# Four split buffers, four opening quarters, a queue of its own for the first weights, and the last two value units made 512 wide

## The chip, the cores and the metric

The kernel runs on one core of a Trainium2 chip. The time is that of one execution on the device, in microseconds (us); less is better. Engines are named as in the profile: PE (TensorE, matrix products), DVE (VectorE), ACT (ScalarE), POOL (GpSimd), SP (SyncE, which issues the transfers).

## What is computed

One decoder layer over 256 tokens of width 1024, in float32, and a last RMS norm:

```python
def layer(h, mem):
    u = rms_norm(h, norm_mix)
    z = u @ w_in                                   # 1024 x 3328
    y_rwkv = rwkv7_time_mix(z[:, :1792], ...)      # 8 heads x 64, a recurrence over tokens, group norm, gate
    q, k, v = split(z[:, 1792:], 3)
    y_moba = causal_softmax_attention(q, k, v)     # 8 heads x 64 (one block of 256 tokens)
    h = h + concat([y_rwkv, y_moba]) @ w_mix_out
    q = rms_norm(h, norm_xattn) @ w_xq             # 4 heads x 256
    k, v = split(rms_norm(mem, norm_mem) @ w_xkv, 2)
    h = h + softmax(q @ k.T / 16) @ v @ w_xo
    a = square(relu(rms_norm(h, norm_ffn) @ w_ff1))   # 1024 x 4096
    h = h + a @ w_ff2
    return rms_norm(h, norm_final)
```

## The kernel before, in words

**Split products.** Each weight product is made of three matmuls of rounded operands: high x high, high x low and low x high. A weight goes through three places: a transfer brings a unit of 1 MB into one of three `raw` buffers (`load_unit`, SP); ACT rounds half a unit, 128x1024, into `w_hi` (`split_hi`); DVE subtracts it from the original to get `w_lo` (`split_lo`). There are `NSPLIT` = 3 such pairs, used in turn: half `s` can be rounded only when half `s - 3` has been multiplied (`dense_mm`).

**Units and quarters.** `units()` lists the 65 units in the order in which they are loaded: `z` (input projection of the recurrence), `mq` and `mv` (attention), `xk` and `xw`, `xv` (keys and values of the cross-attention), `mix` (w_mix_out), `xq`, `xo`, `f1`, `f2`. PE works in quarters of a unit, 260 in all, in the order of `QUARTERS`; 12 matmuls of 256 columns, or 6 of 512 in the `WIDE` units. The letter a below stands for the first half of the inner dimension and b for the second. The first two units of `mix`, of `xo` and of `f1` are interleaved: two quarters that need only the part of the input which is ready early come first, and the ones that need the late part (`dve_gate`, `dve_values`, `dve_op`) behind them.

**Order on each engine.** Each engine has one instruction stream, written out by hand: `dense(n)` on PE is the next n quarters, `split()` on ACT and DVE the next half, and between them stand the steps of everything else. The recurrence goes through `lora`, `rates`, `sums`, `key_sums`, `key_norm`, `decays`, `keys`, `tails`, `tokens`, `bonus`, `mats`, `invert`, `cross`, `join`, `solve`, `outq`, `phi`, `psi`, `state`, `states_out`, `deviation`, `head_root`, `normalize` and `gate`; the attention through `pair_...`; the cross-attention through `scores`, `weigh`, `turn`, `values`. `take(o)` is DVE's emptying of an output's PSUM bank, `operand(what, j)` the rounding of two of the eight slices of the input of the next product (ACT high, DVE low), `rms` the norm. `load(0, q)` transposes a quarter of x and `first_hi`/`first_lo` split the first unit by quarters. From the first `f1` unit on, ACT's and DVE's streams follow from the quarters by a rule.

## Time and profile before

| | |
|---|---|
| three runs | 479.34, 481.86, 481.69 us; median 481.69 us |
| profiled execution, time | 479.82 us |
| its span (first to last instruction) | 477.7 us |
| mean granted clock of PE | 0.998 |
| PE busy | 452.7 us (95%) |
| DVE busy | 321.8 us (67%) |
| ACT busy | 246.5 us (52%) |
| a split, half a unit | ACT L992 1.05 us, DVE L1314 1.25 us (means of 128) |
| `operand`, one of two instructions | ACT L1033 0.50 us, DVE L1403 0.75 us (means of 16) |
| an emptying: h (L1357), `xw` (L1364), half an `xv` (L1370) | 0.68, 0.75, 0.47 us |
| `sums` (L1475, L1477) | 2.28 and 1.23 us |

PE carries the products without a break in most of the span; a product's issue is the thing to look at, since a matmul's shown length overlaps the next one's. The span begins with the loading of x and ends with the last norm and the stores.

### The profile page before, as it was taken

The numbers are of one execution on the slowest core, as the hardware profiler recorded it, in microseconds if no ns is written. First come the engines' busy times: TensorE is split into PE (matmuls) and PEld (weight loads), VectorE is DVE, ScalarE is ACT, GpSimd is POOL, SyncE is SP. The second block draws the span as 40 slices with busy tenths as digits, with TensorE's granted clock in tenths as the row PEclk, the third lists the DMA queues.
The fourth block names the chain that finished last, engine by engine and source line by source line (L and its number), as shares of the span: only waits on it lengthen the run. The fifth ranks groups of instructions, "written<-read, shape, count | busy, mean of one in ns | idle before, by whom it ended". The sixth has DMA issues, their size and how long they took to land.

```text
span 477.7 us, 10346 instructions
## 1 busy us (share of the span) xinstructions
PE 452.7 (95%) x4390; PEld 404.3 (85%) x4390; DVE 321.8 (67%) x475; ACT 246.5 (52%) x396; POOL 35.2 (7%) x54
## 2 busy tenths in 40 slices
PE   4999999999899999899999997999999999999995
PEld 3999999878788888899998995888888888888883
DVE  3667899985567948569476367575747575666656
ACT  4799944245464446337344344555544354544444
POOL 8300000000000000052000053000000000000000
PEclk9999999999999999999999999999999999999999
DMA  8953464222422415454443155446565746657412
GB/s 247 308 186 114 151 195 149 92 92 80 124 93 89 126 59 170 137 171 159 153 155 111 50 144 160 157 140 231 177 196 161 245 151 217 199 197 230 142 69 88
DMA packets 59937, 73.05 MB, mean 153 GB/s; under 512 B 1378, under 2 KB 48564, under 8 KB 59892
## 3 DMA queue, kind: packets, MB, share of 16 engines
q1 hardware_dynamic: 59812, 72.14, 46.7%
q8 instruction: 35, 0.57, 0.5%
q0 software_dynamic: 80, 0.26, 0.2%
q14 instruction: 10, 0.08, 0.1%
HBM read 71.35 MB, written 1.05 MB: 152 GB/s over the span
## 4 chain that ended last, share of the span: by engine, by line
PE 71%; DVE 12%; ACT 5%; issue 3%; ACTq 0%; DVEq 0%
PE bank L542 9%; PE bank L556 7%; PE bank L558 7%; PE bank L557 7%; PE bank L593 6%; PE bank L595 6%; PE bank L594 6%; PE bank L540 5%; DVE w_lo L1314 4%; DVE op L1403 2%; PE bank L573 2%; ACT w_hi L992 2%; PE bank L575 2%; PE bank L574 2%; PE bank L917 2%
## 5 line engine op out<-in xcount | busy, mean ns | idle before, releaser
L1314 DVE TENSOR_TENSOR w_lo<-raw,w_hi 128x1024 fp32r<-128x1024 f32 x128 | 158.9, 1251 | 76.6 <-ACT w_hi L992 76.3
L992 ACT ACTIVATE w_hi<-raw 128x1024 fp32r<-128x1024 f32 x128 | 133.2, 1054 | 70.1 <-PE bank L558 28.2
L556 PE MATMUL bank<-op,w_hi 128*128 128x256 f32 x416 | 121.4, 292 | 4.5 <-DVE w_lo L1314 2.8
L558 PE MATMUL bank<-op,w_lo 128*128 128x256 f32 x416 | 117.8, 283 | 1.1 <-issue 1.1
L557 PE MATMUL bank<-op,w_hi 128*128 128x256 f32 x416 | 117.6, 283 | 0.0
L556 PEld LDWEIGHTS bank<-op,w_hi 128*128 128x128 f32 x416 | 79.5, 191 | 7.6 <-issue 6.2
L558 PEld LDWEIGHTS bank<-op,w_lo 128*128 128x128 f32 x416 | 79.6, 191 | 1.5 <-issue 1.5
L542 PE MATMUL bank<-op,w_hi 128*128 128x512 f32 x224 | 80.0, 396 | 0.0
L557 PEld LDWEIGHTS bank<-op,w_hi 128*128 128x128 f32 x416 | 79.7, 191 | 0.2
L540 PE MATMUL bank<-op,w_lo 128*128 128x256 f32 x256 | 66.4, 280 | 0.1
L540 PEld LDWEIGHTS bank<-op,w_lo 128*128 128x128 f32 x256 | 48.3, 189 | 2.9 <-DVE op L1403 0.4
L593 PE MATMUL bank<-w_hi,op 128*128 128x512 f32 x128 | 50.0, 391 | 0.4 <-DVE w_lo L1314 0.4
L595 PE MATMUL bank<-w_hi,op 128*128 128x512 f32 x128 | 49.8, 389 | 0.0
L594 PE MATMUL bank<-w_lo,op 128*128 128x512 f32 x128 | 49.8, 389 | 0.0
L542 PEld LDWEIGHTS bank<-op,w_hi 128*128 128x128 f32 x224 | 42.1, 188 | 8.6
L1041 ACT ACTIVATE op<-s 128x512 fp32r<-128x512 f32 x16 | 10.1, 632 | 42.4 <-DVE s L1417 42.4
L593 PEld LDWEIGHTS bank<-w_hi,op 128*128 128x128 f32 x128 | 24.0, 188 | 5.8 <-issue 0.8
L595 PEld LDWEIGHTS bank<-w_hi,op 128*128 128x128 f32 x128 | 24.0, 188 | 5.1
L594 PEld LDWEIGHTS bank<-w_lo,op 128*128 128x128 f32 x128 | 24.0, 188 | 5.0
L1420 DVE TENSOR_TENSOR op<-s,op 128x512 fp32r<-128x512 f32 x16 | 11.1, 693 | 11.2 <-ACT op L1041 11.2
L539 PE MATMUL bank<-op,w_hi 128*128 128x512 f32 x32 | 13.1, 410 | 3.3 <-DVE w_lo L1314 2.0
L1050 ACT ACTIVATE s<-bank 128x256 f32<-128x256 f32 x32 | 10.9, 372 | 8.3 <-PE bank L542 8.3
(258 smaller groups left out, 606.4 us busy)
## 6 DMA issues: line engine op xcount, KB each, us to landing
raw<-in_w_ff SPq DMA_DIRECT2D x32, 1024.0 KB, 5.5
raw<-in_w_in SPq DMA_DIRECT2D x12, 1024.0 KB, 5.4
raw<-in_w_xkv SPq DMA_DIRECT2D x8, 1024.0 KB, 5.3
raw<-in_w_mix_out SPq DMA_DIRECT2D x4, 1024.0 KB, 5.0
raw<-in_w_xq SPq DMA_DIRECT2D x4, 1024.0 KB, 5.0
raw<-in_w_xo SPq DMA_DIRECT2D x4, 1024.0 KB, 4.9
xval<-in_x SPq DMA_DIRECT2D x4, 256.0 KB, 4.8
raw<-in_w_in SPq DMA_DIRECT2D x4, 256.0 KB, 5.5
```

The source lines that it names most:

```text
L539: mm(pair(b[:, :]), wh[:, k, :], op[0][:, :, k, :], start=True, stop=False)
L540: mm(b[:, 0:T], wl[:, k, :], op_hi[0][:, k, :], start=False, stop=False)
L542: last = mm(pair(b[:, :]), wh[:, k, :], op[0][:, :, k, :], start=False, stop=final)
L556: mm(dst, wh[:, k, :], op_hi[which][:, k, :], start=first, stop=False)
L557: mm(dst, wh[:, k, :], op_lo[which][:, k, :], start=False, stop=False)
L558: last = mm(dst, wl[:, k, :], op_hi[which][:, k, :], start=False, stop=final)
L593: mm(dst[:, :], hi, wh[:, k, :], start=first, stop=False)
L594: mm(dst[:, :], hi, wl[:, k, :], start=False, stop=False)
L595: last = mm(dst[:, :], lo, wh[:, k, :], start=False, stop=final)
L992: op(view(w_hi), r, ACT.Copy).then_inc(hi_done, 1)
L1314: tt(view(w_lo), r, view(w_hi).bitcast(f32), ALU.subtract).then_inc(lo_done, 1)
L1420: tt(op_lo[1][:, k:k + 2, :], pair(sq), op_hi[1][:, k:k + 2, :].bitcast(f32), ALU.subtract).then_inc(dve_hidden, 1)
```

## The change

The change does five things. The four transfers of the first unit are issued by ACT instead of SP. `NSPLIT` becomes 4; the room comes from `tmp`, half of `rinv` and `center`, which move into buffers that are free at the time. The three opening pairs of units take four early quarters before the first late one, with PSUM room for four half outputs (`half_of_out`). The two `xv` units, one ahead of `mix` and one behind it, become two `xx` units of 512 columns, both behind `mix`. POOL squares the new h after `operand` instead of after `take`. The streams of PE, ACT and DVE are written anew around this.

```diff
-NRAW, NSPLIT = 3, 3
+NRAW, NSPLIT = 3, 4
...
-    out += [("xv", "w_xkv", 0, D + 512, 2)]
     out += [("mix", "w_mix_out", 0, 256 * j, j) for j in range(4)]
-    out += [("xv", "w_xkv", 0, D + 256 * j, j) for j in range(3, 4)]
+    out += [("xx", "w_xkv", 4 * j, D + 512, j) for j in range(2)]
...
-WIDE = ("mv", "xw")
+WIDE = ("mv", "xw", "xx")
...
-        QUARTERS += [(2 * _u + _i, _late ^ _p ^ 1) for _i, _p in
-                     ((0, 0), (2, 0), (0, 1), (1, 0), (1, 1), (2, 1), (3, 0), (3, 1))]
+        QUARTERS += [(2 * _u + _i, _late ^ _p ^ 1) for _p in range(2) for _i in range(4)]
...
+        def half_of_out(o, i):
+
+            what, j = OUTS[o][3:5]
+            if i and j < 2 and what in ("mix", "xo"):
+                return B[{"mix": 4, "xo": 2}[what] + j][:, 0:T]
+            return dense_bank[o % 2][:, i * T:i * T + T]
...
-                sp.dma_start(first_to[:, k, :], first[:, k, UNITS[0][3]:UNITS[0][3] + 256]).then_inc(first_in[i], 16)
...
-                    pool.wait_ge(out_taken, FIRST[what] + j + 1)
+                    if what == "mix":
+                        pool.wait_ge(dve_op, op_no("mix", j) + 1)
+                    elif j == 0:
+                        pool.wait_ge(dve_op, op_no("xo", 3) + 1)
...
-            params(0); load(0, 0); load(0, 1); load(0, 2); dense(1); load(0, 3); dense(2); params(1); dense(1)
-            spread(0); dense(4); lora(); dense(9); key_sums(); dense(4); spread(1); dense(12); load(1, 0)
-            dense(2); tokens(); load(1, 1); dense(1); bonus(); values_turn(); dense(1); mats(0); dense(2)
...
+            params(0); load(0, 0); load(0, 1); dense(1); load(0, 2); dense(1); load(0, 3); dense(2); params(1)
+            spread(0); dense(8); lora(); dense(8); key_sums(); dense(2); spread(1); dense(11); load(1, 0)
+            tokens(); dense(1); load(1, 1); bonus(); values_turn(); dense(1); mats(0); dense(1); load(1, 2)
...
-            pair_scores(2); state(2); dense(4); pair_turn(2, 0); pair_turn(2, 1); state(3); pair_values(2)
...
-            pair_turn(3, 1); states_out(); dense(2); deviation(); dense(4); gate(); dense(3); pair_values(3)
-            dense(22); rms(2); dense(6); scores(0); dense(3); scores(1); turn(0); dense(2); values(0); turn(1)
...
+            pair_turn(3, 0); pair_turn(3, 1); states_out(); dense(2); deviation(); dense(3); pair_values(3)
+            gate(); dense(30); rms(2); dense(4); scores(0); dense(2); scores(1); turn(0); dense(2); values(0)
...
+            for i in range(4):
+                k = slice(2 * i, 2 * i + 2)
+                act.dma_start(first_to[:, k, :], first[:, k, UNITS[0][3]:UNITS[0][3] + 256]).then_inc(first_in[i], 16)
             act.wait_ge(pool_const, 1)
...
+                    if j < 2:
+                        tt(h[:, 0, :], half_of_out(o, 0), h[:, 0, :], ALU.add)
+                        tt(h[:, 1, :], half_of_out(o, 1), h[:, 1, :], ALU.add).then_inc(out_taken, 1)
+                        return
                     tt(h, src, h, ALU.add).then_inc(out_taken, 1)
```

The quarters stand so on PE. At `mix`, before: mix0 first half b, mix1 first half b, then mix0 first half a, which waits for the gates. Now: both halves of mix0 and of mix1 with b, and then the four with a. `xo` and `f1` are built alike, with a first and b late. In front of the gates PE had 76 quarters and two early ones of `mix`; now it has 72 and four. `tokens` stood behind quarter 34 and stands behind quarter 32, `mats(0)` behind 36 and now behind 34, `deviation` behind 71 and now behind 70.

**ACT, the opening.** The first instructions of ACT before (L1063 and L983 are `load(0, q)` with `first_hi(q)`, L1084 and L1090 are `stats(0)`, L992 is a `split`, L1073 is `copies`):

```order
L970 ACT_TABLE_LOAD
L970 ACTIVATE small<-eps 128x1
...
L1063 ACTIVATE op0<-bank2,par 128x256 x2
L983 ACTIVATE w_hi<-raw 128x512
L1063 ACTIVATE op0<-bank3,par 128x256 x2
L983 ACTIVATE w_hi<-raw 128x512
L1084 ACTIVATE neu,row_sum<-xval 128x1024 x2
L1090 ACTIVATE row_sum<-row_sum,eps 128x2
L992 ACTIVATE w_hi<-raw 128x1024
L1073 ACTIVATE hT<-bank0 128x512
```

And now, where L1066, L986, L1087, L1093, L995 and L1076 are the same in turn:

```order
L970 DMA raw<-in_w_in 128x2x256 x4
L973 ACT_TABLE_LOAD
L973 ACTIVATE small<-eps 128x1
...
L1066 ACTIVATE op0<-bank2,par 128x256 x2
L986 ACTIVATE w_hi<-raw 128x512
L1076 ACTIVATE hT<-bank0 128x512
L1076 ACTIVATE hT<-bank1 128x512
L1066 ACTIVATE op0<-bank3,par 128x256 x2
L986 ACTIVATE w_hi<-raw 128x512
L1087 ACTIVATE neu,row_sum<-xval 128x1024 x2
L1093 ACTIVATE row_sum<-row_sum,eps 128x2
L995 ACTIVATE w_hi<-raw 128x1024 x2
```

The four transfers stand first, and the copies of the first two quarters of x have moved from behind `stats(0)` to ahead of the last quarter's rounding.

**DVE, from the norm of the recurrence to the gates.** Before (L1648 and L1651 are `normalize`, L1657 is `gate`, L1661 is `gate_low`, L1686 is `pair_values(3)`, L1370 empties the first `xv` unit, L1364 an `xw` output):

```order
L1364 TENSOR_SCALAR xval<-bank,row_sum 128x512
L1314 TENSOR_TENSOR w_lo<-raw,w_hi 128x1024
L1648 SCALAR_TENSOR_TENSOR s<-s,par 128x256 x4
L1651 TENSOR_TENSOR s<-s 128x1024
L1657 TENSOR_TENSOR s<-bank,s 128x512 x2
L1314 TENSOR_TENSOR w_lo<-raw,w_hi 128x1024
L1661 TENSOR_TENSOR op<-s,op 128x512
L1314 TENSOR_TENSOR w_lo<-raw,w_hi 128x1024
L1686 TENSOR_TENSOR op<-bank,op 128x256
L1370 TENSOR_SCALAR xval<-bank,row_sum 128x256 x2
L1314 TENSOR_TENSOR w_lo<-raw,w_hi 128x1024
L1661 TENSOR_TENSOR op<-s,op 128x512
```

And now (L1374 empties an `xw` output, L1651 and L1654 are `normalize`, L1689 `pair_values(3)`, L1660 `gate`, L1664 `gate_low`, L1319 a split, L1363 and L1364 empty mix0):

```order
L1374 TENSOR_SCALAR xval<-bank,row_sum 128x512
L1651 SCALAR_TENSOR_TENSOR s<-s,par 128x256 x4
L1654 TENSOR_TENSOR s<-s 128x1024
L1689 TENSOR_TENSOR op<-bank,op 128x256
L1319 TENSOR_TENSOR w_lo<-raw,w_hi 128x1024
L1660 TENSOR_TENSOR s<-bank,s 128x512
L1374 TENSOR_SCALAR xval<-bank,row_sum 128x512
L1660 TENSOR_TENSOR s<-bank,s 128x512
L1319 TENSOR_TENSOR w_lo<-raw,w_hi 128x1024 x2
L1664 TENSOR_TENSOR op<-s,op 128x512 x2
L1363 TENSOR_TENSOR hT<-bank,hT 128x256
L1364 TENSOR_TENSOR hT<-bank,hT 128x256
```

`normalize` no longer stands behind the second emptying of `xw` and a split, `pair_values(3)` has moved ahead of the gates, and the emptying of `xv` is gone from here.

**DVE, from the last `xo` outputs into `f1`.** Before (L1357 empties an `xo` output into hT, L1403 is the low part of `operand`, L1314 is a split):

```order
L1314 TENSOR_TENSOR w_lo<-raw,w_hi 128x1024
L1357 TENSOR_TENSOR hT<-bank,hT 128x512
L1314 TENSOR_TENSOR w_lo<-raw,w_hi 128x1024
L1403 SCALAR_TENSOR_TENSOR op<-hT,par,op 128x256 x2
L1314 TENSOR_TENSOR w_lo<-raw,w_hi 128x1024
L1357 TENSOR_TENSOR hT<-bank,hT 128x512
L1314 TENSOR_TENSOR w_lo<-raw,w_hi 128x1024
L1403 SCALAR_TENSOR_TENSOR op<-hT,par,op 128x256 x2
L1314 TENSOR_TENSOR w_lo<-raw,w_hi 128x1024
```

And now (L1366, L1406 and L1319 are the same in turn):

```order
L1319 TENSOR_TENSOR w_lo<-raw,w_hi 128x1024 x2
L1366 TENSOR_TENSOR hT<-bank,hT 128x512
L1319 TENSOR_TENSOR w_lo<-raw,w_hi 128x1024
L1406 SCALAR_TENSOR_TENSOR op<-hT,par,op 128x256 x2
L1319 TENSOR_TENSOR w_lo<-raw,w_hi 128x1024
L1366 TENSOR_TENSOR hT<-bank,hT 128x512
L1319 TENSOR_TENSOR w_lo<-raw,w_hi 128x1024
L1406 SCALAR_TENSOR_TENSOR op<-hT,par,op 128x256 x2
L1319 TENSOR_TENSOR w_lo<-raw,w_hi 128x1024 x3
```

The order reads much alike; what differs is which half each split is. Ahead of the emptying of the last `xo` output (the second L1366) the first two halves of `f1` are now split, where before it was the first alone; the third follows between that emptying and its operand, and the fourth right behind the operand.

## Rows read from the trace of the kernel before

**Rows 1.** The page, part 1: busy time of each engine

```profile
PE 452.7 (95%) x4390; PEld 404.3 (85%) x4390; DVE 321.8 (67%) x475; ACT 246.5 (52%) x396; POOL 35.2 (7%) x54
```

**Rows 2.** Busy time by stretch: us, PE, PEld, DVE, ACT, POOL, clock, DMA

```profile
40.00:60.00 20.00, 19.12 (x150) 18.60 (x151) 14.50 (x22) 19.35 (x27) 0.00 (x0) 1.00 0.38 115
60.00:80.00 20.00, 19.73 (x160) 19.18 (x159) 19.79 (x26) 8.60 (x15) 0.00 (x0) 1.00 0.44 149
```

**Rows 3.** Timeline of PE: start, length, line, operation; products of 256 columns

```profile
199.84 0.28 PE L558 MATMUL bank<-op,w_lo 128*128 128x256 f32 x1
199.96 0.28 PE L556 MATMUL bank<-op,w_hi 128*128 128x256 f32 x1
```

**Rows 4.** Timeline of PE, products of 512 columns (unit `xw`)

```profile
173.12 0.40 PE L575 MATMUL bank<-w_hi,op 128*128 128x512 f32 x1
173.35 0.40 PE L573 MATMUL bank<-w_hi,op 128*128 128x512 f32 x1
```

**Rows 5.** Timeline, the opening; in brackets idle time before and its releaser

```profile
6.05 0.88 DVE L1445 SCALAR_TENSOR_TENSOR op<-bank,par,op 128x256 fp32r<-128x256 f32 x2 [2.03 <-ACT op L1063]
...
8.92 1.12 PE L643 MATMUL bank<-ident,xval 128*128 128x128 f32 x4 [1.70 <-DMA xval<-in_x]
...
12.39 1.06 PE L643 MATMUL bank<-ident,xval 128*128 128x128 f32 x4
...
13.49 0.84 ACT L1063 ACTIVATE op<-bank,par 128x256 fp32r<-128x256 f32 x2 [2.06 <-PE bank L643]
...
19.94 0.36 PE L556 MATMUL bank<-op,w_hi 128*128 128x256 f32 x1 [0.58 <-DVE w_lo L1314]
```

**Rows 6.** Transfers, moved GB in the first 8 us, in 40 slices

```profile
GB/s 0 0 0 0 0 0 0 0 0 82 195 205 169 241 236 256 190 282 358 353 287 225 195 210 210 246 287 205 174 164 195 225 241 282 277 287 307 312 333 333
```

**Rows 7.** Timeline of PE, where it stood between 38 and 100 us

```profile
40.24 0.35 PE L556 MATMUL bank<-op,w_hi 128*128 128x256 f32 x1 [0.50 <-DVE w_lo L1314]
52.13 0.36 PE L556 MATMUL bank<-op,w_hi 128*128 128x256 f32 x1 [0.64 <-DVE w_lo L1314]
...
98.83 1.29 PE L768 MATMUL bank<-neu,X 32*32 32x32 f32 x128 [0.75 <-DVE neu L1592]
```

**Rows 8.** Timeline of DVE (`tails`) and PE (`tokens`)

```profile
68.92 2.35 DVE L1514 TENSOR_TENSOR s<-s,pend 128x1024 f32<-128x1024 f32 x2
...
71.59 1.91 PE L706 MATMUL bank<-ident,s 128*128 128x128 f32 x16
```

**Rows 9.** Timeline, the gates and the opening of `mix`

```profile
182.82 0.75 DVE L1364 TENSOR_SCALAR xval<-bank,row_sum 128x512 f32<-128x512 f32 x1 [0.83 <-PE bank L575]
...
192.22 0.36 PE L556 MATMUL bank<-op,w_hi 128*128 128x256 f32 x1 [0.98 <-DVE op L1686]
...
194.13 0.36 PE L556 MATMUL bank<-op,w_hi 128*128 128x256 f32 x1 [0.25 <-DVE w_lo L1314]
```

**Rows 10.** Timeline, the first quarter of `xq`

```profile
219.99 2.31 DVE L1314 TENSOR_TENSOR w_lo<-raw,w_hi 128x1024 fp32r<-128x1024 f32 x1
...
222.56 0.36 PE L556 MATMUL bank<-op,w_hi 128*128 128x256 f32 x1 [0.84 <-DVE w_lo L1314]
```

**Rows 11.** Timeline, the last heads of the cross-attention and the opening of `xo`

```profile
256.94 1.35 PE L917 MATMUL bank<-xkey,zT 128*128 128x256 f32 x5 [0.35 <-DVE zT L1386]
...
267.65 0.39 PE L556 MATMUL bank<-op,w_hi 128*128 128x256 f32 x1 [0.70 <-DVE op L1706]
```

**Rows 12.** Timeline, the opening of `f1`

```profile
287.16 0.28 PE L558 MATMUL bank<-op,w_lo 128*128 128x256 f32 x1
...
288.68 0.47 PE L539 MATMUL bank<-op,w_hi 128*128 128x512 f32 x1 [1.25 <-ACT w_hi L992]
...
292.01 2.69 DVE L1403 SCALAR_TENSOR_TENSOR op<-hT,par,op 128x256 fp32r<-128x256 f32 x2
...
292.34 0.47 PE L539 MATMUL bank<-op,w_hi 128*128 128x512 f32 x1 [2.02 <-DVE w_lo L1314]
```

**Rows 13.** Timeline, the first `f2` unit

```profile
319.69 0.47 PE L593 MATMUL bank<-w_hi,op 128*128 128x512 f32 x1 [0.36 <-DVE w_lo L1314]
```

More of the change, by code:

```diff
@@ L1277, in _ @@
-            split(); operand('mix', 3); split(); rms(2); split(); split(); scores(0); split(); split(); turn(0)
-            scores(1); split(); split(); values(0); turn(1); scores(2); split(); values(1); turn(2); split()
-            scores(3); values(2); turn(3); values(3); split(); split(); split(); split(); follow(29); follow(30)
-            split(); follow(31); split(); split()
+            load(0, 0); load(0, 1); load(0, 2); copies(0); load(0, 3); stats(0); split(); split(); follow(0)
+            split(); split(); copies(1); stats(1); gates(); follow(1); split(); split(); split(); split()
@@ new lines, in _ @@
+            pair_values(3); split(); split(); gate(0); gate(1); split(); split(); split(); split(); split()
+            split(); split(); operand('mix', 0); operand('mix', 1); split(); split(); split(); operand('mix', 2)
+            operand('mix', 3); split(); split(); split(); rms(2); split(); split(); scores(0); turn(0)
+            scores(1); values(0); split(); turn(1); split(); split(); scores(2); values(1); split(); turn(2)
+            split(); scores(3); values(2); turn(3); values(3); split(); split(); follow(29); follow(30); split()
@@ L1281, in _ @@
+            split(); split(); split(); follow(31)
             at[0] = PHASE["xo"]
@@ L1283, in _ @@
             rms(3)
-            for i in range(4):
+            for i in range(3):
                 dense(2)
                 residual(i)
+            dense(4)
+            residual(3)
             dense(len(QUARTERS) - at[0])
@@ new lines, in _ @@
+            split(); split(); operand('mix', 1); split(); take(23); operand('mix', 2); split()
+            operand('mix', 3); split(); split(); take(24); take(25); split(); take(26); scores(0); weigh(0)
+            split(); split(); scores(1); take(27); weigh(1); values(0); split(); scores(2); split(); weigh(2)
+            split(); values(1); take(28); scores(3); weigh(3); split(); split(); values(2); values(3); split()
+            take(29); split(); take(30); follow(29); follow(30); split(); split(); take(31); split(); follow(31)
```

163 lines of the change are left out of this document (72 added, 91 removed).

## The prediction

> **What bounds the kernel now.** I read the page's busy times first. PE is busy for 95% of the span, DVE for 67%, ACT for 52% [rows 1]: PE sets the time, and what counts is its work and the places where it stands. Then the table by stretches. Between 40 and 60 us ACT is busy for 19.35 of 20 us, between 60 and 80 us DVE for 19.79 [rows 2]; here the recurrence and the splits fill the helping engines, and PE has little to spare ahead of them. Last the timeline of PE. In a plain run of products one of 256 columns follows the other after 0.12 us [rows 3] and one of 512 columns after 0.23 us [rows 4]. A quarter thus takes 12 x 0.12 = 1.44 us, or 6 x 0.23 = 1.38 us in 512 columns. Any larger step is time that PE lost. The idle time in brackets understates it by the 0.16 us by which a shown length (0.28 us) exceeds the step. With that PE lost 0.66 and 0.80 us to late splits at 40 and 52 us and 0.91 us at 99 us [rows 7], 1.14 and 0.41 us at the opening of `mix` [rows 9], 1.00 us at the first quarter of `xq` [rows 10], 0.51 and 0.86 us in the cross-attention [rows 11], 288.68 - 287.16 - 0.12 = 1.40 us and 2.02 + 0.16 = 2.18 us at the opening of `f1` [rows 12], and 0.52 us at `f2` [rows 13]. That is 10.4 us that a better order could win at most, beside the opening.
>
> **The 512 columns.** The two `xv` units are 96 products at 0.12 us, 11.52 us. As `xx` they are 48 at 0.23 us, 11.04 us. PE's work falls by 0.5 us [rows 3, 4]. DVE has two instructions fewer; it isn't the bound there.
>
> **The opening: 0.** Before, PE's third transposition of x starts at 8.92 us, when its data lands, the fourth at 12.39 us behind a quarter of products, and PE's second unit at 19.94 us. The chain behind the fourth is ACT's: rounding from 13.49 us, the norm's sums, the first split of the second unit, then DVE's part of it [rows 5]. It takes 19.94 - 12.39 = 7.5 us, and it stays. The new order puts two quarters of products ahead of the fourth transposition instead of one. The first can start near 7.0 us, when DVE has rounded the first quarter of x (6.05 + 0.88), if the second transposition is done by then. Here a transposition and a quarter together take 12.39 - 8.92 = 3.5 us, of which I put 0.8 on the transposition. So the fourth starts at 7.0 + 2 x 3.5 - 0.8 = 13.2 us. PE's products speed up later in the opening (a plain quarter is 1.44 us); if that comes earlier too, up to 1.6 us of this go: 11.6 us. If x lands no earlier than now, PE starts 1 us later than assumed, and the chain is 1.8 us late. The rate lies near 200 to 250 GB/s in most slices and rises above 300 in the last [rows 6], when more is queued; with both queues filled from the start it could rise earlier. Bounds: 0.8 us won, 1.8 us lost. I take 0: the speeding up and the delay cancel, and the moved copies fit into an idle time of ACT of 2.06 us [rows 5]. The Trainium skill ("DMA: Bandwidth & Descriptors", rules for kernel authors) says that spreading transfers over issuing engines doesn't help bandwidth and only saves issue time. By that rule the sum would be nearer the lower bound; by the rising rate in the rows it would be near 0. No run here has two queues, so the trace can't decide it.
>
> **From 20 us to the opening of `mix`: -1.0.** The fourth pair of buffers lets ACT round one half further ahead. The two losses at 40 and 52 us, 1.46 us, should go. Against that `tokens` comes two quarters (2.9 us) earlier on PE, and it waits for `tails` on DVE, which ends at 68.92 + 2.35 = 71.27 us, 0.3 us ahead of the transposition [rows 8]. DVE is full there [rows 2], so PE will stand until DVE has come that far. I count the same splits ahead of `tails` on DVE, one emptying less, and `sums` (3.5 us) later than before. The new `tails` ends perhaps 1 us earlier, and PE arrives some 1.5 us too early. That loss is a loan: the two quarters are still there, behind the step. At the far end, the gates: `normalize` stands behind an emptying of `xw` that waited for PE, at 182.82 us [rows 9] and a split of 1.25 us. Without these it starts some 2 us earlier, and behind it DVE no longer empties `xv` (0.9 us) nor splits `xv` ahead of the gates. PE has 76 quarters to reach the first gated one now, and 78 before, and both gates should be ready when it comes: of the 1.14 + 0.41 us, 1.2 goes. Sum of the possible gains, with the 0.91 at 99 us: 3.9 us. What stands against it is the missing filler of two quarters, 2.9 us, if the chain of the recurrence is no faster. I take 1.0 won; the bounds are 3.9 won and 2.9 lost.
>
> **The first quarter of `xq`: -1.0.** Before, 4 quarters of `xv` covered the rounding of h; DVE was late because two of its instructions ran at double length beside POOL's squares (a split took 2.31 us [rows 10], against 1.25 in the mean). Now 8 quarters of `xx`, 11.0 us, lie there, and the squares come behind `operand`. DVE needs 4 x 1.5 us for `operand`, 3 x 0.7 for emptyings and 5 x 1.25 for splits, with ACT's parts ahead of them; the latest of it is due when `xq` reaches the second half of the inner dimension, at 12.5 us, and I find it done at 11.8. The norm (`rms(2)`) comes 4 quarters later than before, but so does the first `scores`. Without this cover the 1.0 would stay.
>
> **Cross-attention and `xo`: -0.9.** `xo` now needs the last heads after 12 quarters from the first `scores` instead of 11, so the 0.86 us goes. The 0.51 us, a wait for the emptying of the last `xq` output [rows 11], stays at about 0.4.
>
> **The opening of `f1`: -3.4.** This is the largest term. Call E the end of `xo`. Before, the second half ready for PE came at 292.34 us, since three splits, an emptying and an operand stood in DVE's line and the third buffer was taken. Now two halves of `f1` are split before E, and four quarters (4 x 1.4 = 5.6 us) need no late operand. In DVE's line follow emptying until E + 0.9, the third split until E + 2.2 (due at E + 2.8), the operand until E + 3.0 (due at E + 5.6), and the fourth split until E + 4.2 (due at E + 4.2). So 0 to 0.3 us remains of 1.40 + 2.18 = 3.6. POOL's squares, beside which the operand took 2.69 us instead of 1.5 [rows 12], have moved behind it. Lower bound of the gain 1.4, if the fourth split is late by two.
>
> **`f2`: -0.4** of the 0.52 us [rows 13], with a half more in hand. The halved emptyings of `mix` and `xo` cost DVE 0.1 us each, beside products; if DVE were the bound, 0.4 in all.
>
> **The sum** is 0.5 + 0 + 1.0 + 1.0 + 0.9 + 3.4 + 0.4 = 7.2 us. The profiled execution took 479.82 us, so it would be 472.6. That execution lies 1.9 us below the median of the three runs, 481.69; taken from the median the same sum gives 474.5. I put the forecast between, at 473.5 us.
>
> **The rivals.**
> *All of the early part is won too* (0.15). If the chain of the recurrence moves with PE, all 3.9 us of that stretch go, and the opening gives 0.8: 473.5 - 2.9 - 0.8 = 470. For it: PE was the one waited for at 182.82 us [rows 9]. Against it: DVE at 99% from 60 to 80 us [rows 2].
> *The early steps stall PE and it isn't paid back* (0.17). `tokens`, `spread(1)` and `cross` stand earlier on PE than DVE and ACT can serve them, 2.9 us lost and 1.1 in the opening: 473.5 + 1.0 + 2.9 + 1.1 = 478.5. For it: the 0.3 us in [rows 8] and ACT at 97% from 40 to 60 us.
> *Slower* (0.06). `sums` on DVE moves behind the sixth unit, and ACT's `decays` and all behind it wait for it. From the second stretch on every step is tied to this chain; if it ends at the gates more than 8.4 us later than before, PE stands there for longer than the 6.2 us won behind and the 1.0 counted here. With 10 us late: 485. Against it: ACT's work up to `decays` is the same, and it was nearly without a gap.
> *The late gains fail* (0.07): at `f1` the fourth split and at `xq` the operands stay late, and 3 us of the 6 are lost: 476.5.
>
> **Chances and range.** Forecast 0.55. The forecast's own range is 471 to 476. The range over the cases goes from 468, below the rival that wins all, to 478.5. Half a per cent, 2.4 us, is about what a measurement of this kernel can tell from no change. Faster, below 479.3: 0.55 + 0.15 + 0.07 and most of the 0.17, 0.86; within: 0.08; slower: 0.06.
>
> **What would show it.** In the new profile: step 0.23 us in `xx`; PE's second unit starting at 19 to 21 us; no lost time at 40 and 52, but a wait of PE for DVE at `tokens`; `mix` opening without a wait of over 0.4 us, near 187 to 191 us; no wait at `xq`; at `f1` two splits of DVE ahead of the last emptying, and PE without a gap. The prediction is wrong if PE's idle time between 20 and 190 us grows, or if the gap at `f1` remains.

## The result and the profile after

The changed kernel takes 474.80 us in the median of 4 runs (473.48 to 477.06), the kernel before 480.61 us in 4 (479.34 to 481.86). The ratio is 0.987, with a 95% interval of 0.984 to 0.991: faster, by 1.3%. The profiled execution took 473.48 us, 6.3 less than the one of before, with a span of 471.8 us. The forecast was 473.5 us.

The page of the changed kernel, busy times, to be read against [rows 1]:

```profile
PE 449.3 (95%) x4342; PEld 400.5 (85%) x4342; DVE 316.6 (67%) x477; ACT 245.1 (52%) x395; POOL 36.3 (8%) x54
```

The 48 products fewer are the 96 of `xv` that became 48. To see where the rest went I compare when PE starts the quarter of the same number (from 0) in both timelines; the first 92 hold four `xv` quarters before and four of `mix` now. The second column is the change of that distance within the stretch; the terms of the forecast stand beside it.

| stretch, up to quarter | forecast | measured | start before, after |
|---|---|---|---|
| opening, up to 4 (second unit) | 0 | +1.0 | 19.94, 20.94 |
| up to 92 | -1.0 | -2.0 | 210.04, 209.05 |
| `xx` and `xq`, up to 105 | -1.5 | +0.1 | 230.68, 229.81 |
| cross-attention and `xo`, up to 131 | -0.9 | -1.3 | 285.84, 283.69 |
| `f1`, up to 147 | -3.4 | -3.4 | 315.06, 309.48 |
| `f2`, up to 155 | -0.4 | -0.3 | 326.90, 320.98 |
| the rest, up to 259 | 0 | 0.0 | 470.20, 464.26 |
| sum | -7.2 | -5.9 | |

The timeline of the changed kernel at the places of [rows 5, 7, 8, 10 and 12], one engine after the other (start, length, engine, line; in brackets idle time before and its releaser). The opening:

```profile
5.33 0.24 PE L618 MATMUL bank<-ident,prob 8*128 8x8 f32 x1 [5.33 <-DMA prob<-in_norm_mix]
...
13.51 0.60 PE L638 MATMUL bank<-ident,xval 128*128 128x128 f32 x4
...
14.47 0.86 ACT L1066 ACTIVATE op<-bank,par 128x256 fp32r<-128x256 f32 x2
...
20.94 0.35 PE L550 MATMUL bank<-op,w_hi 128*128 128x256 f32 x1 [0.58 <-DVE w_lo L1319]
```

The fourth transposition starts at 13.51 us instead of 12.39, and the chain behind it still takes 7.4 us. PE's first instruction now waits until 5.33 us for a transfer of 4 KB.

`spread(1)`, the end of `tails` on DVE and `tokens` on PE:

```profile
52.27 0.71 PE L651 MATMUL bank<-probT,ones 128*128 128x128 f32 x4 [1.37 <-DVE probT L1460]
...
67.42 2.35 DVE L1517 TENSOR_TENSOR s<-s,pend 128x1024 f32<-128x1024 f32 x2
...
69.83 0.88 PE L701 MATMUL bank<-ident,s 128*128 128x128 f32 x6
```

The two waits for splits in [rows 7] are gone, and a new one for `sums` and the diagonal stands at 52 us. `tails` ends at 69.77 us instead of 71.27, and PE takes up `tokens` 0.06 us behind it.

`xq`, where the forecast saw no wait, DVE and then PE:

```profile
218.24 1.12 DVE L1406 SCALAR_TENSOR_TENSOR op<-hT,par,op 128x256 fp32r<-128x256 f32 x2
...
220.41 2.68 DVE L1406 SCALAR_TENSOR_TENSOR op<-hT,par,op 128x256 fp32r<-128x256 f32 x2
...
223.15 0.39 PE L550 MATMUL bank<-op,w_hi 128*128 128x256 f32 x1 [0.75 <-DVE op L1406]
...
227.41 1.13 PE L661 MATMUL bank<-s,ones 128*128 128x256 f32 x4 [0.40 <-POOL s L468]
```

The old wait of [rows 10] is gone. In its place PE loses 0.91 us waiting for the last `operand` and 0.56 us waiting for POOL. The last `operand` takes 2.68 us, the one before it 1.12.

`f1`, DVE and PE:

```profile
285.94 1.22 DVE L1319 TENSOR_TENSOR w_lo<-raw,w_hi 128x1024 fp32r<-128x1024 f32 x1
287.07 0.88 DVE L1406 SCALAR_TENSOR_TENSOR op<-hT,par,op 128x256 fp32r<-128x256 f32 x2
287.95 1.23 DVE L1319 TENSOR_TENSOR w_lo<-raw,w_hi 128x1024 fp32r<-128x1024 f32 x1
...
285.13 0.40 PE L531 MATMUL bank<-op,w_hi 128*128 128x512 f32 x1
...
289.33 0.46 PE L531 MATMUL bank<-op,w_hi 128*128 128x512 f32 x1
```

PE takes four quarters 1.40 us apart, with no wait. The `operand` beside which POOL's squares stood takes 0.88 us, where it took 2.69 [rows 12].

### The profile page after: what moved, and what is told of

It is laid out like the page before. It is cut to its first block, busy times and chain, and to the rows that moved or that the text cites. A ratio compares the mean times of both kernels' runs of the same rounds, so it can differ in the third digit from the quotient of the medians.

```text
span 471.8 us, 10246 instructions
## 1 busy us (share of the span) xinstructions
PE 449.3 (95%) x4342; PEld 400.5 (85%) x4342; DVE 316.6 (67%) x477; ACT 245.1 (52%) x395; POOL 36.3 (8%) x54
## 4 chain that ended last, share of the span: by engine, by line
PE 48%; DVE 1%; ACT 1%; POOL 1%; issue 1%; ACTq 0%; POOLq 0%
PE bank L534 10%; PE bank L587 6%; PE bank L589 6%; PE bank L588 6%; PE bank L532 6%; PE bank L551 3%; PE bank L550 3%; PE bank L552 3%; PE bank L531 2%; PE bank L912 2%; PE bank L933 2%; DVE w_lo L1319 1%; POOL s L468 0%; ACT w_hi L995 0%; POOL s L467 0%
## 5 line engine op out<-in xcount | busy, mean ns | idle before, releaser
L1319 DVE TENSOR_TENSOR w_lo<-raw,w_hi 128x1024 fp32r<-128x1024 f32 x128 | 155.1, 1232 | 67.3 <-ACT w_hi L995 67.0
L995 ACT ACTIVATE w_hi<-raw 128x1024 fp32r<-128x1024 f32 x128 | 132.1, 1054 | 56.1 <-PE bank L552 31.1
L534 PE MATMUL bank<-op,w_hi 128*128 128x512 f32 x224 | 79.9, 396 | 0.0
L587 PE MATMUL bank<-w_hi,op 128*128 128x512 f32 x128 | 49.9, 390 | 0.3 <-ACT xval L1245 0.3
L589 PE MATMUL bank<-w_hi,op 128*128 128x512 f32 x128 | 49.8, 389 | 0.0
L1053 ACT ACTIVATE s<-bank 128x256 f32<-128x256 f32 x32 | 11.1, 376 | 24.5 <-PE bank L534 24.5
L567 PE MATMUL bank<-w_hi,op 128*128 128x512 f32 x48 | 19.9, 414 | 0.0
```

The costliest lines, as they stand in the source:

```text
L534: last = mm(pair(b[:, :]), wh[:, k, :], op[0][:, :, k, :], start=False, stop=final)
L567: mm(b[:, :], hi, wh[:, k, :], start=(xk == 0), stop=False)
L587: mm(dst[:, :], hi, wh[:, k, :], start=first, stop=False)
L589: last = mm(dst[:, :], lo, wh[:, k, :], start=False, stop=final)
L995: op(view(w_hi), r, ACT.Copy).then_inc(hi_done, 1)
L1319: tt(view(w_lo), r, view(w_hi).bitcast(f32), ALU.subtract).then_inc(lo_done, 1)
```

## The experiments

Each ran beside the kernel before on the same chip, and the ratio is to that kernel; the changed kernel itself ran on the same chip only beside four buffers alone, the transfers held back and POOL at once, so small differences to it are read by stage. Times are medians; where a stage is compared, it is the start of the same quarter in the timelines, one profile of each kernel. In all of them only the order or the place of work changes; everything is still computed.

**The changed kernel again**, to see what differs between executions of it.

> The changed kernel once more, unedited. In its first profile PE lost 0.49 us in the middle of the small products of the state (at 134.6 us) and 1.22 us behind them, at full clock; in all four variants profiled since, PE stood there for 2.3 to 2.7 us with nothing in the profile to wait for, while two units of weights were landing, and the granted clock then fell to half for some 3 us. Theory A (PE's instructions are fetched late beside the two transfers, which falls out one way or the other from execution to execution): the stop appears in this kernel too, and where it does the mean clock of the run is about 0.995 and the span 473.5 to 475; where it doesn't, 0.998 and 472. Rival B (the edits of the variants caused it): every execution is like the first profile, span 471.8 to 472.5.

476.56 us (473.81 to 478.28, 6 runs); ratio 0.988 [0.983, 0.992]. Theory A holds for the stop, which now appears in the unedited kernel, and it matters more than any term of the forecast but one; the spans go further apart than it said (472.1 to 476.5 us). The stretches of this profile (us, PE, PEld, DVE, ACT, POOL, clock, DMA share, GB/s):

```profile
135.00:136.00 1.00, 1.00 (x69) 0.87 (x70) 1.00 (x2) 0.10 (x1) 0.00 (x0) 1.00 1.08 386
136.00:137.00 1.00, 0.75 (x70) 0.61 (x55) 0.97 (x3) 0.00 (x0) 0.00 (x0) 1.00 1.15 381
137.00:138.00 1.00, 0.00 (x0) 0.00 (x0) 0.54 (x2) 0.00 (x0) 0.00 (x0) 1.00 1.00 354
138.00:139.00 1.00, 0.00 (x0) 0.00 (x0) 0.00 (x0) 0.00 (x0) 0.00 (x0) 1.00 1.05 393
139.00:140.00 1.00, 0.86 (x79) 0.86 (x83) 0.00 (x0) 0.00 (x0) 0.00 (x0) 1.00 0.37 137
140.00:141.00 1.00, 1.00 (x57) 0.93 (x45) 0.00 (x0) 0.36 (x1) 0.00 (x0) 0.79 0.14 43
141.00:142.00 1.00, 1.00 (x7) 1.00 (x7) 0.00 (x0) 1.00 (x3) 0.00 (x0) 0.50 0.00 0
142.00:143.00 1.00, 1.00 (x6) 1.00 (x6) 0.44 (x2) 1.00 (x5) 0.00 (x0) 0.50 0.00 0
```

PE stops in the middle of the small products of `psi`, and ACT and DVE soon after it, while the transfers run at 350 to 390 GB/s. When PE comes back the granted clock goes from 1.00 to 0.50, that is from 2.4 to 1.2 GHz. The same stop in PE's timeline:

```profile
139.14 0.21 PE L831 MATMUL bank<-U,btok 32*64 32x64 f32 x1 [2.38 <-issue]
```

"issue" means that PE waited for nothing that the profile shows: no semaphore, no tile. What it lacked stands in the view of the transfers, queue by queue. In this profile, from 133.0 to 136.4 us:

```profile
q1 hardware_dynamic: 964, 0.99, 92.7%
...
raw<-in_w_xkv SPq DMA_DIRECT2D x1, 1024.0 KB, 7.0
```

From 136.4 to 139.2 us:

```profile
q1 hardware_dynamic: 547, 1.02, 101.3%
q8 instruction: 1, 0.02, 2.5%
q14 instruction: 1, 0.01, 1.1%
```

And in the first profile of the changed kernel, from 131 to 134 us:

```profile
q1 hardware_dynamic: 767, 0.79, 84.5%
q8 instruction: 1, 0.02, 5.3%
```

A queue called "instruction", q8, moves packets of 16 KB during the run, 34 in the span, on the engines that carry the weights (a second one of this kind, q14, has ten packets of 8 KB). In the first profile the packet began at 131.18 us, as the weights began to fill the engines, and PE stood 0.28 us. Here it began only at 136.55 us, 7.3 us after the one before it, though the fetches before it are 3.5 to 5.3 us apart. `psi` is a run of 224 small products, each with its weight load, and PE runs out of instructions. That PE waits for this packet shows in every profile: in all 13 together PE has 28 "issue" stops of over 0.45 us between 100 and 150 us, and after each of them it starts again 1.2 to 1.6 us after a 16 KB packet of q8 has ended (here 137.69 and 139.14 us). The stop and the half clock behind it put PE back against the first profile, from 1.92 us at quarter 54 to 4.22 at quarter 57: 2.3 us, though the first profile loses 1.7 there itself. The four variants profiled before this one (norm's row first, one queue, `f1` by two quarters, roundings first) show the same stop, of 2.10 to 2.47 us; in them the packet began 7.0 to 7.5 us after the one before it. The clock was also at 0.50 from 21.1 to 24.5 us here, behind PE's stand ahead of the second unit; from quarter 4 to 8 PE takes 7.13 us instead of 5.82.

**The two transfers held back.** Units 16 and 17 are issued 2.3 us apart at 130 us, just ahead of `psi`.

```diff
             for u in range(2, len(UNITS)):
+                if u == 16:
+                    sp.wait_ge(pe_psi, 2)
                 load_unit(u)
```

> The changed kernel with one wait more on SP: the transfer of unit 16 (and 17 behind it) is issued when PE has done the last of those small products, some 6 us later than now; both are split 5.9 and 9.2 us after they land now. Theory A: with no bulk transfer beside them the stop inside the small products shrinks to what the kernel before shows there (0.8 to 1.0 us) or less, the clock stays at 1.00, and all spans are 471.5 to 472.5, so the median falls by 1 to 2 us against the changed kernel. Rival B: the stop is there whatever is being transferred, nothing changes. Rival C: the later landing makes the splits of unit 16 late, and PE loses at 144 us what it won at 135.

473.01 us (471.60 to 474.17, 6 runs), ratio 0.982 [0.978, 0.986]: 3.5 us below the changed kernel beside it (3.2 by the means; the six runs of each scatter by 2.6 and 4.5 us). The stretches of its profile:

```profile
134.00:135.00 1.00, 1.00 (x114) 1.00 (x105) 0.97 (x3) 0.00 (x0) 0.00 (x0) 1.00 0.00 0
135.00:136.00 1.00, 1.00 (x78) 0.93 (x64) 0.41 (x2) 0.16 (x1) 0.00 (x0) 1.00 0.06 16
136.00:137.00 1.00, 1.00 (x10) 1.00 (x10) 0.00 (x0) 1.00 (x3) 0.00 (x0) 1.00 0.04 7
137.00:138.00 1.00, 1.00 (x8) 0.80 (x7) 0.27 (x1) 1.00 (x5) 0.00 (x0) 1.00 0.70 152
138.00:139.00 1.00, 1.00 (x11) 1.00 (x10) 0.88 (x4) 1.00 (x6) 0.00 (x0) 1.00 1.07 378
```

The stop is gone altogether, the clock stays, and the later landing costs nothing: rivals B and C fall. Even against the first profile, where the stop was short, it is 1.85 us ahead at quarter 58. The same packet of q8 now runs from 131.03 to 132.23 us, with no weights beside it. Its other executions still show mean clocks down to 0.992, so this isn't the only place where the clock falls.

**Four buffers alone**, in the kernel before (the small tensors moved as in the change; the diff is that of the change for `NSPLIT`, `tmp`, `rinv` and `center`).

> The kernel before with four split buffers and the moves of the small tensors that make room for them, and nothing else: the order of the quarters, the value units and the opening are as before. Theory D (the buffers are what wins at f1, since two opening quarters there cost the four-buffer kernel nothing): the two stops at the opening of f1, 1.40 and 2.18 us, shrink to under 1 us in all, those at 40 and 52 us go (1.46 us), and the time is 3.5 to 5.5 us below the kernel before, 475 to 477. Rival E (buffers and four opening quarters are needed together): the stops at f1 stay within 1 us of what they were, and the time is 478.5 to 480.

476.31 us (475.82 to 478.56, 6 runs), ratio 0.989 [0.985, 0.993]. By the profiles it is 0.3 us behind the kernel before at quarter 131, wins 2.4 us at `f1` and 0.9 at `f2`, and is 3.05 ahead at the last quarter. The first of the two stops at `f1` is gone, the second shrinks from 2.18 to 1.31 us:

```profile
290.26 0.47 PE L541 MATMUL bank<-op,w_hi 128*128 128x512 f32 x1 [1.15 <-DVE w_lo L1316]
```

So the buffers do most of it at `f1`, though 1.31 us remain where theory D had under 1; the waits at 40 and 52 us stay at 0.66 and 0.81 us. That part of theory D was wrong. The reason may be that ACT's written order has no split to spare there; no run shows it.

Two things more stand in this run. Its median is 5.2 us below the kernel before beside it, a ratio of 0.989, where the whole change has 0.987 and 0.988: in the median the other four parts of the change together won nothing that can be told from noise. (The profile shows 3.05 of the 5.2 us; where the rest lies is not shown.) And its SP issues units of weights at 122.2 and 137.9 us, as the kernel before does at 122.4 and 137.2, and not at 130.1 and 132.3 like the changed kernel. It isn't the fourth buffer that moved these transfers onto `psi`, but the new order of the splits on DVE.

**`f1` opened by two quarters** in the changed kernel, as before the change.

```diff
+    if UNITS[_u][4] == 0 and UNITS[_u][0] == "f1":
+        QUARTERS += [(2 * _u + _i, _late ^ _p ^ 1) for _i, _p in
+                     ((0, 0), (2, 0), (0, 1), (1, 0), (1, 1), (2, 1), (3, 0), (3, 1))]
-    if UNITS[_u][4] == 0 and _late is not None:
+    elif UNITS[_u][4] == 0 and _late is not None:
```

> The changed kernel with the first two f1 units opened as before the change: two early quarters, then the late ones (the order of these 8 quarters alone is put back; four buffers, the order on DVE and ACT and POOL's place stay). The change won 3.6 us at this place. Theory A: most of that is the fourth buffer with the two splits ahead of the last emptying, and POOL out of the way; the third split is then ready 2.2 us behind the end of xo, and PE, which wants it after one quarter (1.4 us), stands for 0.8 us; no wait for the last operand. Loss against the changed kernel 0.8 to 1.2 us. Theory B: the four early quarters carry the gain; without them PE stands for the third split and the last operand as before, loss 2.5 to 3.6 us, 0.6 to 0.7%.

475.82 us, ratio 0.991 [0.989, 0.993]; by the profiles the distance to the changed kernel comes up at `psi` (0.74 us at quarter 54, 3.08 at 57), from the stop. Within `f1` its distance to the changed kernel goes from 3.09 us at quarter 131 to 2.96 at quarter 148. It loses 0.88 us behind the first quarter, and gets it back as the later ones come:

```profile
290.50 0.47 PE L534 MATMUL bank<-op,w_hi 128*128 128x512 f32 x1 [0.71 <-DVE w_lo L1322]
```

With the fourth buffer there, the four early quarters of `f1` are worth nothing.

**POOL squares at once**, for `mix` and `xo`, as before the change.

```diff
-                    if what == "mix":
-                        pool.wait_ge(dve_op, op_no("mix", j) + 1)
-                    elif j == 0:
-                        pool.wait_ge(dve_op, op_no("xo", 3) + 1)
+                    pool.wait_ge(out_taken, FIRST[what] + j + 1)
```

> The changed kernel with POOL squaring a pair of the new h as soon as it is emptied, as before the change, instead of behind its rounding. In the profile of the changed kernel the last pair of DVE's roundings took 2.68 us beside POOL's products, against 0.87 us alone, and PE lost 0.91 and 0.56 us in xq. Theory F (POOL's products slow DVE wherever they fall, so their place only moves the cost): the long DVE instructions move to the emptyings and splits behind mix, PE's first quarter of xq starts within 0.8 us of the changed kernel's after the end of mix (11.0 us after the first quarter of xx), and the median stays within 1 us. Rival G (the new place is what keeps xq clear): PE loses 1 us or more again at the first quarter of xq.

475.53 us, ratio 0.986 [0.982, 0.990], 1.0 us below the changed kernel beside it. The total hides two opposite effects: from quarter 99 to 104 it gains 1.67 us on the changed kernel, and at `f1` it loses 2.05. Neither theory had both. DVE at `xq`, then DVE and PE at `f1`:

```profile
220.41 0.86 DVE L1403 SCALAR_TENSOR_TENSOR op<-hT,par,op 128x256 fp32r<-128x256 f32 x2
...
222.33 0.87 DVE L1403 SCALAR_TENSOR_TENSOR op<-hT,par,op 128x256 fp32r<-128x256 f32 x2
...
287.73 2.69 DVE L1403 SCALAR_TENSOR_TENSOR op<-hT,par,op 128x256 fp32r<-128x256 f32 x2
...
291.70 0.47 PE L528 MATMUL bank<-op,w_hi 128*128 128x512 f32 x1 [1.87 <-DVE w_lo L1316]
```

At `mix` POOL is done before the last roundings begin; behind `operand` its work on one pair falls on the rounding of the next. At `xo` it is the reverse.

**The roundings of `mix` ahead of the splits** in the changed kernel (first ACT's order, then DVE's; `take(23)` empties the output whose bank `xq` needs).

```diff
-            split(); split(); operand('mix', 0); operand('mix', 1); split(); split(); split(); operand('mix', 2)
-            operand('mix', 3); split(); split(); split(); rms(2);
+            split(); split(); operand('mix', 0); operand('mix', 1); operand('mix', 2); operand('mix', 3)
+            split(); split(); split(); split(); split(); split(); rms(2);
...
-            split(); split(); operand('mix', 1); split(); take(23); operand('mix', 2); split()
-            operand('mix', 3); split(); split(); take(24);
+            split(); operand('mix', 1); split(); operand('mix', 2); operand('mix', 3); split(); take(23); split()
+            split(); split(); take(24);
```

> The changed kernel with operands 2 and 3 of mix moved forward: on ACT right behind operands 0 and 1, on DVE ahead of the emptying of the first xx output, which waits for PE. In the changed kernel DVE stood 1.17 us for that emptying, operand 3 ended at 223.1 us beside POOL's squares (2.68 us for two instructions instead of 0.87 us each pair), PE lost 0.91 us in xq0's third quarter and 0.56 us at rms(2), waiting for POOL. Theory A: the emptying ahead of operand 2 is the cause of both; with the operands moved PE has no gap over 0.3 us between the start of xx and the first scores, and the time falls by 1.2 to 1.5 us, 0.3%. Theory B: POOL beside DVE is the cause; the operands then still take twice their length, splits of xx come late instead, and PE loses 0.5 us or more in xx or xq.

476.99 us, ratio 0.992 [0.990, 0.995]. The total alone can't be told from the changed kernel's, but the stage is worse: from quarter 99 to 105 it loses 0.76 us on the changed kernel. DVE and PE:

```profile
217.60 4.27 DVE L1406 SCALAR_TENSOR_TENSOR op<-hT,par,op 128x256 fp32r<-128x256 f32 x4
...
224.81 0.39 PE L550 MATMUL bank<-op,w_hi 128*128 128x256 f32 x1 [2.17 <-DVE xval L1374]
```

The four instructions of operands 2 and 3 now all run beside POOL, 1.07 us each where one alone takes 0.44, and the emptying behind them is what `xq` waits for. Theory B holds: DVE's order wasn't the fault; POOL's place was.

**One queue** for the first transfers, as before, and **the norm's row first**, each in the changed kernel. In the first, SP issues each quarter of the first unit behind its quarter of x, and ACT none.

```diff
-                act.dma_start(first_to[:, k, :], first[:, k, UNITS[0][3]:UNITS[0][3] + 256]).then_inc(first_in[i], 16)
+                sp.dma_start(first_to[:, k, :], first[:, k, UNITS[0][3]:UNITS[0][3] + 256]).then_inc(first_in[i], 16)
```

> The changed kernel with the four transfers of the first unit issued by SP again, between those of x, as before the change; the order on PE, ACT and DVE stays the changed one. Theory A (the second queue costs time): norm_mix lands at 3.5 us again, PE starts there, the first quarter of products starts at 7.5 to 8.0 us (8.52 in the changed kernel), and the second unit at 20.0 to 20.5 us instead of 20.94. Theory B (the second queue pays, the order on PE costs): the last quarter of x lands at 10.4 us instead of 9.5, its rounding is later, and the second unit starts at 21.5 us or later. In the time: 0.1 to 0.2% less than the changed kernel by A, 0.1% more by B.

> The changed kernel with the 4 KB transfer of norm_mix issued ahead of the first quarter of x on SP, and nothing else. In the changed kernel PE's first instruction waited for this transfer until 5.33 us (3.49 us before the change), and PE's second unit started at 20.94 us instead of 19.94. Theory A: the small transfer landed late because the first quarters of x and of the weights, now issued side by side, were under way ahead of it; issued first it lands before the first quarter of x does (4.6 us), PE starts at 4.7 to 5.0 us, and the second unit at 20.2 to 20.6 us, 0.3 to 0.7 us earlier. Time 0.1% less than the changed kernel. Theory B: the late start of the second unit comes from the order on PE (two quarters ahead of the fourth transposition) and not from the start; the second unit stays at 20.8 us or later.

One queue: 474.27 us (473.84 to 474.83, 4 runs), ratio 0.987 [0.985, 0.990]; the second unit starts at 20.26 us. The norm's row ahead of x: 475.53 us, 0.990 [0.987, 0.992]; the second unit starts at 20.78. PE's first instruction and the second unit with one queue:

```profile
3.58 0.24 PE L621 MATMUL bank<-ident,prob 8*128 8x8 f32 x1 [3.58 <-DMA prob<-in_norm_mix]
...
20.26 0.36 PE L553 MATMUL bank<-op,w_hi 128*128 128x256 f32 x1 [0.58 <-DVE w_lo L1317]
```

The queue of its own costs 0.7 us, by one profile; the seven profiles with the changed opening whole have this start at 20.64 to 21.60 us. The row first brings nothing that can be told from this scatter: PE's first instruction starts at 2.71 us, but the transposition behind it waits until 5.27 us for x, and neither theory's range was met. It isn't bandwidth that the second queue costs. In the first 12 us the changed kernel, and then the one with one queue, moved:

```profile
DMA packets 3399, 3.27 MB, mean 273 GB/s; under 512 B 214, under 2 KB 3355, under 8 KB 3399
...
DMA packets 2992, 2.91 MB, mean 243 GB/s; under 512 B 140, under 2 KB 2992, under 8 KB 2992
```

With two queues the eight transfers of x and of the first unit have all landed by 9.5 us, with one by 11.0. But the two that PE begins with come later: the row at 5.2 us instead of 3.4 and the first quarter of x at 4.6 instead of 3.6, so the first quarter of products starts at 8.52 us instead of 7.79.

**The whole opening of before** in the changed kernel: one queue (edit as above), and PE's and ACT's order.

```diff
-            params(0); load(0, 0); load(0, 1); dense(1); load(0, 2); dense(1); load(0, 3); dense(2); params(1)
+            params(0); load(0, 0); load(0, 1); load(0, 2); dense(1); load(0, 3); dense(2); params(1); dense(1)
...
-            load(0, 0); load(0, 1); load(0, 2); copies(0); load(0, 3); stats(0); split(); split(); follow(0)
+            load(0, 0); load(0, 1); load(0, 2); load(0, 3); stats(0); split(); copies(0); split(); follow(0)
```

> The changed kernel with the opening of the kernel before: all first transfers from SP, PE doing the third transposition of x ahead of the first quarter of products, ACT copying behind the norm's sums. The changed kernel's second unit starts at 20.9 us (20.6 to 21.6 in three profiles) against 19.94 and 19.57 before, and with one queue alone it was 20.26. Theory A (the new queue costs 0.7 and the new order 0.3): the second unit starts at 19.5 to 20.0 us, and later stretches follow by the same amount as far as PE sets them. Since PE stands for less time ahead of the second unit (0.6 to 0.8 us instead of 1.6), the granted clock should no longer fall to half at 21 to 25 us, as it did in two of the profiles; median 1 us or more below the changed kernel. Rival B (the chain of the recurrence on DVE and ACT sets the start of tokens): what is won in the opening is gone again at tokens, near 70 us, and the median is within 0.5 us of the changed kernel's.

473.48 us (471.92 to 474.91), ratio 0.984 [0.980, 0.987]. The second unit starts 1.19 us earlier than in the changed kernel, and PE stands 0.81 us ahead of it instead of 1.55:

```profile
18.49 0.68 PE L654 MATMUL bank<-prob,ones 128*128 128x128 f32 x4 [0.81 <-DVE one_k_a L1433]
...
19.75 0.35 PE L553 MATMUL bank<-op,w_hi 128*128 128x256 f32 x1 [0.58 <-DVE w_lo L1317]
```

At quarter 35, behind `tokens`, the 1.19 us are all there: DVE and ACT moved along with PE, and rival B falls. At quarter 57 0.72 is left, where an "issue" stop of 1.62 us falls (the changed kernel has one of 1.06 there), and 0.75 at the last quarter. The clock stays at 1.00 behind the second unit, but so it does in seven of the nine profiles that stand there for 1.55 us; this run doesn't show that the shorter stand is what keeps it.

**`tokens` one quarter later** in the changed kernel.

```diff
-            tokens(); dense(1); load(1, 1); bonus(); ...
+            dense(1); tokens(); load(1, 1); bonus(); ...
```

> The changed kernel with quarter 33 ahead of tokens on PE instead of behind. PE waits some 0.7 us for DVE at tokens now, at 69.8 us. The prediction's reading (a loan: the quarter stands behind the step instead): the wait there vanishes, tokens comes 0.7 to 0.8 us later, and at quarter 36 PE is within 0.8 us of where it is now, so the time stays within 1 us. Rival (the early tokens is what lets the chain of the recurrence run ahead): everything from quarter 36 on is 0.7 us later or more up to mix.

474.02 us (473.49 to 476.73), ratio 0.986 [0.982, 0.989]. Quarter 36 starts at 85.96 us instead of 86.33, quarter 44 at 102.29 instead of 102.33. The wait is gone and nothing is lost or won: it was a loan.

**Three together**: the opening of before, the transfers held back, and POOL at once for `mix` but behind the rounding for `xo` (the edit below; the others are as above).

```diff
                     if what == "mix":
-                        pool.wait_ge(dve_op, op_no("mix", j) + 1)
+                        pool.wait_ge(out_taken, FIRST[what] + j + 1)
```

> The changed kernel with three things: the opening of the kernel before, the two transfers held back until the small products of the state are done, and POOL squaring the h of mix at once but that of xo behind its rounding. If the three add up: 3.5 us for the transfers (measured), 1.7 us at xq (measured, with the 2.0 us it cost at f1 avoided), 0 to 1 for the opening: 468 to 470.5 us in the median, 5 to 7 us below the changed kernel and 11 to 13 below the kernel before. If the gain at xq or in the opening ends in a wait further on, 471 to 473.

469.35 us (468.13 to 470.27, 6 runs), ratio 0.975 [0.972, 0.978] to the kernel before. The last quarter starts at 460.37 us, where the changed kernel has 464.26 and 468.49 in its two profiles. The three add up by stage: against the first of these it is 2.19 us ahead at quarter 92, gains 1.67 more by quarter 104, and loses nothing at `f1`. This version beats both kernels: 11.9 us below the kernel before beside it, and about 5 to 7 below the changed one, which ran on other chips.

## Why the prediction was right, and where it wasn't

**The total** came out within 1.3 us of the median, though two terms were wrong, and partly by luck: the opening and `xq` fell short by 1.0 and 1.6 us, the stretch to `mix` and the cross-attention gave 1.0 and 0.4 more than their terms, and the second set of runs of the same kernel has 476.56. In the profiled execution the sum of the stretches is -5.9 us against the forecast of -7.2.

**The 512 columns, -0.5**: right. The 8 quarters of `xx` take 220.09 - 209.05 = 11.04 us.

**The opening, 0**: wrong, it was +1.0, inside the bounds given. The step that failed is the cancelling of speed-up and delay. The first quarter of products was to start near 7.0 us and started at 8.52, 1.5 us late, and PE's earlier speed-up gave back 1.2 of it: the fourth transposition stands at 13.51 us, 0.3 behind the 13.2 of the sum without any speed-up, and the chain of 7.4 us hangs on it. With two queues the transfers of the first unit land earlier, but the first of x and the small row land later, and PE begins with these. By single profiles 0.7 us belong to the queue and 0.5 to the order. The Trainium skill ("DMA: Bandwidth & Descriptors", rules for kernel authors) has the rule that I had set against the term, that spreading transfers over issuing engines doesn't help bandwidth and only saves issue time. The sum came out as by that rule, but not by its reason: the rate rose, from 243 to 273 GB/s in the first 12 us, with SP's issues of x done by 3.2 us instead of 4.7. Whether the earlier issue is all of that rise isn't shown.

**20 us to `mix`, -1.0**: -2.0 in the first profile. The waits at 40 and 52 us went as expected, but not by the fourth buffer, which alone leaves them; whether the new order of ACT and DVE would do it with three buffers wasn't run. In their place PE stands for 1.37 us at `spread(1)`. `tokens` was a loan, as said. `mix` opens without a wait. By my own sign the stretch is no clean hit: from PE's second unit to 190 us PE's idle time grew, from 4.9 to 5.4 us (6.1 in the second profile), and 1.55 us were won at the opening of `mix`, behind it. The 3.9 us of possible gains also don't add up as written: with 1.2 us for `mix` they are 3.6. What I missed is the stop in `psi`. In the kernel before, units were fetched at 122 and 137 us, on either side of these products; with DVE's splits bunched at 129 to 132 us by the new order, two fetches fall right onto them. In five of nine profiles with the transfers there, PE stood for over 2 us; with them held back the spread of six runs narrows from 4.5 us to 2.6. I had asked what each transfer waits for, not what else uses the engines while it moves.

**`xq`, -1.0**: wrong, about +0.6. The step that failed is that DVE would be done 11.8 us behind the start of `xx`; it was done at 14.0. The sum of DVE's work ahead of `xq` used 1.5 us for each `operand` and no wait. The four took 0.88, 0.87, 1.12 and 2.68 us, by whether POOL ran beside them, which is less in all, but DVE stood for 1.17 us ahead of the emptying of `xx`, and the last, the one that is due, met both of POOL's products. "The squares come behind `operand`" is true of each pair, but each lies on the next pair's rounding. With POOL at once the wait is gone. The Trainium skill ("SBUF — State Buffer", two separate sides) says that a DVE instruction with two SBUF inputs and a GpSimd one that reads SBUF lock their shared ports against each other for a whole instruction. The rows fit that: 0.87 us alone and 2.68 beside POOL's products of 1.89 and 1.34 us, while the emptying at 217.57 us, one of whose inputs is in PSUM, took 0.75 us beside POOL and 0.74 without it (POOL at once, 219.75 us).

**Cross-attention, -0.9**: right, -1.3 with `xo`.

**`f1`, -3.4**: the size was right, and one of its three reasons was not needed. The fourth buffer gives 2.4 of it; POOL's later place is worth 2.0 in the changed kernel (the two sum to more than 3.4, so they overlap); the four early quarters give nothing.

**`f2`, -0.4**: -0.3; with four buffers alone -0.9.

**The rivals.** Of the rival in which the early steps stall PE and it isn't paid back, the 1.0 us lost in the opening came true; the wait at `tokens` was paid back, and the time lost at `psi` is another mechanism, which no rival had. The chain on DVE did not hold the time: what the opening won with its old order was whole at quarter 35, and 0.75 us of 1.19 were left at the last.

## What to carry to other kernels

A new order of the work that frees buffers moves the transfers. Look where the big ones land: a stretch of hundreds of small matmuls needs its instructions fetched, and two units of weights in flight beside it can stop PE for 2.4 us and cost the clock after it. Run the simplest part of a change alone first: here four buffers gave in the median what all five parts gave. When two engines slow each other, placing one behind the other's instruction helps only if the next such instruction isn't due at once. Compare by stage, not by total: here two effects of 1.7 and 2.0 us hid in one that looked like nothing.

## What the runs showed of the hardware

- Instructions are fetched over the transfer engines during the run, in 16 KB packets of their own queue (34 of them). In 13 profiles each of PE's 28 stops of over 0.45 us at 100 to 150 us without a wait in the profile ended 1.2 to 1.6 us after such a packet had ended. With 350 to 390 GB/s of weights in flight one packet began 7.3 us after the one before it, and PE stood for 2.38 us; with the engines idle PE stood for 0.82 us (kernel before), 0.55 (four buffers alone) or not at all. That the weights make the packet late is inferred from its place in time and from the run that moved the transfers; no run moved the packet alone.
- In all five profiles with such a stop of 2.10 us or more, the granted clock went to 0.50 some 0.6 to 1.9 us after PE's return and stayed there for 3.4 us; after the "issue" stops of 0.28 to 1.71 us it stayed at 1.00. In the opening PE stood for 1.54 or 1.55 us ahead of its second unit in nine profiles; in two of them the clock then went to 0.50, at 21.1 and 21.7 us, for 3.4 us, in the other seven it didn't.
- A 4 KB transfer behind one queue's first 256 KB landed in time for PE at 3.58 us; with a second queue filled beside it, at 5.33 us. All of x and the first unit, 2 MB, had landed by 11.0 us with one queue and by 9.5 with two.
- Two DVE instructions that read two SBUF operands (`operand`, 128x256) took 0.87 us alone, and 2.68 us beside POOL's products, which read SBUF too; POOL's product took 1.89 us there, and 1.04 while DVE stood idle (POOL at once, 209.11 us).
